# Linear attention's scores by 32-row products, state steps between projection products, and 32-column latent tiles in the first expert stage

## The reference, cut to what matters

```python
cum = jnp.cumsum(lc, axis=1)
inter = jnp.einsum('bchk,bhkv->bchv', qc * jnp.exp(cum), state)
scores = jnp.einsum('bihk,bjhk,bijhk->bhij', qc, kc, jnp.exp(diff))   # causal
intra = jnp.einsum('bhij,bjhv->bihv', scores, vc)
state = jnp.exp(last)[..., None] * state + jnp.einsum('bjhk,bjhv->bhkv', kc * jnp.exp(last[:, None] - cum), vc)
```

```python
hid = jax.nn.silu(jnp.einsum('becd,edf->becf', xs, w_gate)) * jnp.einsum('becd,edf->becf', xs, w_up)
y = jnp.einsum('becf,efd->becd', hid, w_down) * g[..., None].astype(h.dtype)
```

## Time and profile before

| | |
|---|---|
| median of 3 runs | 2052.12 us (2050.4 to 2054.34) |
| the profiled execution, its own time | 2049.58 us |
| its span | 2047.8 us |
| PE busy | 1906.9 us (93%) |
| DVE, ACT, POOL busy | 543.6, 461.7, 158.0 us |
| mean granted PE clock | 0.982 |
| first layer's experts (584 to 1130 us) | PE busy throughout |
| second layer's experts (1571 to 2030 us) | DMA at 426 to 427 GB/s |
| chain that ended last | PE 80%, DMA 11%, DVE 6% |

### The profile page before, as it was taken

The page is one execution under the profiler, slowest core; times in us unless marked ns, Lnnn a source line. Parts: engine busy times, 40 slices in busy tenths (PEclk is TensorE's granted clock), DMA queues, the critical chain, the costliest instruction groups (busy, mean ns, idle before and its releaser), DMA issues.

```text
span 2047.8 us, 24796 instructions
## 1 busy us (share of the span) xinstructions
PE 1906.9 (93%) x10438; PEld 880.8 (43%) x10438; DVE 543.6 (27%) x1212; ACT 461.7 (23%) x959; POOL 158.0 (8%) x225
## 2 busy tenths in 40 slices
PE   5999999999899999999999999989996998898886
PEld 3655545664333333333333555556642332332322
DVE  2021476662330000000001403466624010111113
ACT  4132213433311101110111404124432111110112
POOL 0000011110001010101111000011001000000000
PEclk9999999999899999999999999999997999999998
DMA  9312067002489999999999412130039999999996
GB/s 404 117 41 82 29 281 332 27 16 109 180 333 400 416 403 406 393 398 401 405 382 371 165 41 83 41 149 27 4 116 362 427 426 427 427 425 427 426 428 254
DMA packets 54279, 541.78 MB, mean 265 GB/s; under 512 B 6528, under 2 KB 8704, under 8 KB 23216
## 3 DMA queue, kind: packets, MB, share of 16 engines
q1 hardware_dynamic: 36704, 488.82, 57.8%
q0 software_dynamic: 17344, 51.72, 7.7%
q10 hardware_dynamic: 144, 0.01, 0.0%
HBM read 516.80 MB, written 23.72 MB: 264 GB/s over the span
## 4 chain that ended last, share of the span: by engine, by line
PE 80%; DMA 11%; DVE 6%; ACT 1%; issue 1%; SPq 0%; DVEq 0%; ACTq 0%
PE ps L2059 17%; PE ps L1670 10%; PE ps L2141 9%; PE ps L1895 7%; PE ps L2067 6%; PE ps L1646 5%; DMA ring<-in_wstream 5%; DMA work<-in_wstream 3%; DMA big<-in_wstream 3%; PE ps L1843 3%; PE ps L2148 3%; PE ps L2013 2%; PE ps L1593 2%; PE ps L1781 2%; PE ps L1638 1%; PE ps L1816 1%
## 5 line engine op out<-in xcount | busy, mean ns | idle before, releaser
L2059 PE MATMUL ps<-ring,work 128*64 128x512 f32 x1536 | 341.6, 596 | 14.3 <-DMA ring<-in_wstream 11.7
L1506 DVE TENSOR_TENSOR work<-glao,ps 128x512 f32<-128x512 f32 x31 | 21.3, 687 | 782.0 <-ACT glao L921 408.9
L1670 PE MATMUL ps<-hT,ring 128*128 128x512 f32 (+1 forms) x592 | 209.7, 513 | 4.9 <-issue 2.6
L2059 PEld LDWEIGHTS ps<-ring,work 128*64 128x64 f32 x1536 | 108.9, 137 | 241.5 <-issue 225.8
L2141 PE MATMUL ps<-big,work 128*64 128x512 f32 x704 | 164.7, 605 | 2.1 <-ACT work L881 2.1
L1670 PEld LDWEIGHTS ps<-hT,ring 128*128 128x128 f32 x592 | 113.2, 192 | 99.8 <-issue 89.9
L1895 PE MATMUL ps<-ring,hT 128*128 128x512 f32 x320 | 138.8, 592 | 0.0
L2067 PE MATMUL ps<-ring,work 128*32 128x512 f32 x1024 | 119.6, 597 | 0.0
L1646 PE MATMUL ps<-ring,hT 128*128 128x384 f32 (+3 forms) x384 | 110.9, 450 | 0.0
L736 ACT ACTIVATE work<-ps,work 128x512 f32<-128x512 f32 (+2 forms) x120 | 81.9, 684 | 83.7 <-DVE work L1202 48.5
L2059 PE MATMUL ps<-big,work 128*64 128x512 f32 x384 | 88.3, 605 | 13.3 <-DMA big<-in_wstream 13.3
(11 more groups left out here) (331 smaller groups left out, 2211.8 us busy)
## 6 DMA issues: line engine op xcount, KB each, us to landing
ring<-in_wstream SPq DMA_DIRECT2D x150, 2048.0 KB, 14.0
big<-in_wstream SPq DMA_DIRECT2D x68, 2048.0 KB, 18.7
hT<-in_wstream SPq DMA_DIRECT2D x12, 1024.0 KB, 31.5
work<-in_wstream SPq DMA_DIRECT2D x12, 1024.0 KB, 34.0
x_kept<-big POOLq DMA_DIRECT2D x14, 512.0 KB, 3.0
big<-x_kept POOLq DMA_DIRECT2D x12, 512.0 KB, 5.1
xn_lat<-big POOLq DMA_DIRECT2D x8, 512.0 KB, 3.8
big<-in_x_all SPq DMA_DIRECT2D x6, 512.0 KB, 6.6
```

Of the source, the lines that this page charges most:

```text
L1670: last = T.matmul(bank(n % 4, tn), uw[:, j * D + kc * P:j * D + kc * P + P], hTv[:, kc, t0:t0 + tn], start=kc == 0, stop=kc == KC - 1)
L2059: last = T.matmul(bank(m)[64 * h:64 * h + 64, :], XST[:, kc, e, 0:CAP_L], gate_up[j][kk][:, m * D + h * 512:m * D + (h + 1) * 512], start= ...
```

## The change

- **Scores.** The block-diagonal queries are gone. Per direction and head one product of 32 rows by 128 columns gives the head's scores; head h writes bank h, forward in its first 128 columns and backward in the next 128. `A_SB` has two copies, DVE signals `masked` after the two mask products, and PE starts the scores of the next tile at that signal. PE makes the state part ahead of the next tile's scores, and DVE copies the tile before out after the add. The modulation rows move to banks 4 and 5.
- **State steps.** PE makes state step i and the rotary product i behind item i of unit 4. On DVE a state step, the query arguments of one direction (after the first two steps) and one `rope` follow each other.
- **Ring.** `pe.drain()` and `ring_used` are gone. SP waits for the counters `proj`, `router_in` and `wo` that exist anyway.
- **32-column latent tiles.** In the first layer `up_lat` and `down_lat` make two products of 32 stationary columns in place of each one of 64.

```diff
+        A_SB = [w(GX, 512), w(GX + 1024, 512)]
-        QBLK = [w(q, 512) for q in (0, 512, 1024, GX + 1024)]
...
-                    sp.wait_ge(ring_used[lap(n)[0]], sum(lap(m)[0] == lap(n)[0] and m not in mod_units for m in ring_units if m <= n))
+                if n >= OUT_AT[l]:
+                    sp.wait_ge(sem("wo"), len(tiles(l)) + l * PER["wo"])
+                    return
+                unit = n - IN_AT[l]
+                sp.wait_ge(sem("proj"), n_items(l, unit + 1) + l * PER["proj"])
+                if unit == 2:
+                    sp.wait_ge(sem("router_in"), 1 + l * PER["router_in"])
...
+                for i in range(STEPS):
+                    step(i)
+                    if i < 2:
+                        query_args(l, i)
+                    rope(l, i)
...
-                queries(0)
+                by_head = v3(ps[:, 0:GLA_H * 512], GLA_H)
...
                     if i:
+                        dve.wait_ge(sem("A"), i + l * PER["A"])
+                    for d, (m, dst) in enumerate(((C_MF, A_SB[i % 2]), (C_MB, A_TMP))):
+                        last = V.tensor_tensor(v3(dst, GLA_H), by_head[:, :, d * P:(d + 1) * P],
+                                               cst[:, m:m + P].unsqueeze(1).broadcast_to([P, GLA_H, P]), ALU.mult)
+                    last.then_inc(sem("masked"), 1)
+                    dve.wait_ge(sem("masked"), i + 1 + l * PER["masked"])
+                    V.tensor_tensor(A_SB[i % 2], A_SB[i % 2], A_TMP, ALU.add).then_inc(sem("A"), 1)
...
-                        if unit == 4:
-                            rot(l, n - n_items(l, 4) - 1)
-                pe.drain().then_inc(ring_used[lap(g)[0]], 1)
+                        i = n - n_items(l, 4) - 1
+                        if unit == 4 and i < STEPS:
+                            state(l, i)
+                            rot(l, i)
...
+                    if i:
+                        pe.wait_ge(sem("masked"), i + l * PER["masked"])
                     for d in range(2):
-                        last = T.matmul(bank((4, 0)[i % 2] + d), E[3 * d + 1][:, ts[i] * P:(ts[i] + 1) * P], QBLK[2 * (i % 2) + d],
-                                        start=True, stop=True)
+                        for h in range(GLA_H):
+                            r = slice(DK * h, DK * h + DK)
+                            last = T.matmul(bank(h, P, d * P), E[3 * d + 1][r, c], E[3 * d][r, c], start=True, stop=True)
...
+                block = CAP_C if ctx_too else CAP_L
+                slot_blocks = [(h, b) for h in range(2) for b in range(0, CAP_L, block)]
...
-                                for h in range(2):
-                                    last = T.matmul(bank(m)[64 * h:64 * h + 64, :], XST[:, kc, e, 0:CAP_L],
+                                for h, b in slot_blocks:
+                                    r = CAP_L * h + b
+                                    last = T.matmul(bank(m)[r:r + block, :], XST[:, kc, e, b:b + block],
```

More of the change, by code:

```diff
@@ L1102, in gla_state, with step @@
                 hm = cst[:, C_HM:C_HM + GLA_H]
-                for i in range(NT - 1):
+                def step(i):
                     dve.wait_ge(sem("dS"), i + 1 + l * PER["dS"])
@@ L1114, in gla_state, with rope, query_args @@
                     dve.wait_ge(sem("state"), 2 * i + 2 + l * PER["state"])
[L1116 to L1125, removed]
+                for i in range(STEPS):
[3 more added lines that the diff above has]
+                    rope(l, i)
+            def rope(l, i):
+                b = [SK, SQ, SQ + 1, SQ + 2, SQ + 3][i]
+                dve.wait_ge(sem("rot"), i + 1 + l * PER["rot"])
+                V.tensor_tensor(ROT, bank(6 + i % 2), cst[:, C_SIN:C_SIN + LAT], ALU.mult)
+                link(V.tensor_tensor(FM[:, b, 0:LAT], FM[:, b, 0:LAT], cst[:, C_COS:C_COS + LAT], ALU.mult))
+                V.tensor_tensor(FM[:, b, 0:LAT], FM[:, b, 0:LAT], ROT, ALU.add).then_inc(sem("rope"), 1)
+                dve.wait_ge(sem("rope"), i + 1 + l * PER["rope"])
+            def query_args(l, d):
                 n = width(l)
@@ L1130, in gla_queries @@
                 dve.wait_ge(sem("keT"), 3 + l * PER["keT"])
[L1131 to L1139, removed]
+                c3 = v3(CUM[d], NT)[:, 0:nt, :]
+                mid = c3[:, :, P // 2:P // 2 + 1].broadcast_to([P, nt, P])
+                link(V.tensor_tensor(v3(E[3 * d + 2][:, 0:n], nt), c3, mid, ALU.subtract))
+                V.tensor_scalar(E[3 * d][:, 0:n], E[3 * d + 2][:, 0:n], 80.0, None, ALU.min).then_inc(sem("q_arg"), 1)
+                V.tensor_scalar(E[3 * d + 1][:, 0:n], E[3 * d + 2][:, 0:n], -80.0, -1.0, ALU.max, ALU.mult)\
+                    .then_inc(sem("q_arg"), 1)
+                dve.wait_ge(sem("q_arg"), 3 * d + 2 + l * PER["q_arg"])
+                V.tensor_copy(E[3 * d + 2][:, 0:n], CUM[d][:, 0:n]).then_inc(sem("q_arg"), 1)
+            def gla_queries(l):
+                n = width(l)
                 dve.wait_ge(sem("q_arg"), 6 + l * PER["q_arg"])
-                rope(l)
                 q = FM[:, GQ, 0:n]
@@ L1729, in gla_out @@
                 for i, t in enumerate(ts):
-                    if i + 1 < len(ts):
-                        scores(i + 1)
-                    if i == 0:
-                        mod_cols((1, 5)[l], GLA_ROW, bank(3))
                     c = slice(t * P, (t + 1) * P)
@@ L1926, in w_out @@
                                 last.then_inc(sem("xT"), 1)
-                for j in range(OUT_UNITS):
-                    pe.drain().then_inc(ring_used[lap(OUT_AT[l] + j)[0]], 1)
             def turn_lat(l):
@@ L2138, in down_lat @@
                         for kc in [4 * j + k for k in ks]:
-                            for g in range(2):
+                            for g, b in slot_blocks:
                                 h = g if ctx_too else g ^ e
-                                last = T.matmul(bank(6 if ctx_too else 3)[64 * g:64 * g + 64, :], HT[:, kc, 0:CAP_L],
+                                r = CAP_L * g + b
+                                last = T.matmul(bank(6 if ctx_too else 3)[r:r + block, :], HT[:, kc, b:b + block],
                                                 down[j][kc % 4 // 2][:, kc % 2, h * 512:(h + 1) * 512], start=kc == 0, stop=kc == KC - 1)
```

74 lines of the change are left out of this document (31 added, 43 removed).

## The result

| | before | after |
|---|---|---|
| median | 2051.26 us, 4 runs (2049.97 to 2054.34) | 2013.43 us, 4 runs (2007.03 to 2014.69) |
| profiled execution, its own time | 2049.58 us | 2012.75 us |
| its span | 2047.8 us | 2010.9 us |
| PE, DVE, ACT, POOL busy | 1906.9, 543.6, 461.7, 158.0 us | 1878.4, 531.4, 461.5, 158.0 us |

A forecast was written before the change was run, and what follows sets the result against it. PE was taken to set the pace, except in the second layer's experts (the stream) and where PE waits for DVE. Terms -14.5 - 9.6 - 11.5 - 1.4 = -37.0 us; 2052.1 - 37.0 = 2015, range about 2008 to 2031.

The forecast's parts named there:

- 32-column tiles: First layer's experts: fewer column-width changes between groups, -14.5 us (-15.2 at 0.1067 us per record, -12.8 at 0.1075).
- State steps: Unit 4, both layers: steps behind its items cost 4.3 us and no waiting, -4.8 us per layer, -9.6 in all.
- rival wait: Unit 4: PE waiting for state step i - 2; DVE at most 2 us behind in round 1, within what PE allows.
- Scores: Score tiles, both layers: PE-bound period of 2.8 to 2.9 us against 3.78, -6.8 and -4.9, taken as -11.5 us.
- I take 0.95: A tile's 16 score records: 0.95 us, between 0.73 if columns decide and 1.15 if the number of weight loads does.
- 0.73 us, period 2.6, -14: Better bound for the scores: 16 records in 0.73 us, DVE the limit at a 2.6 us period, -14 us.
- Drains: Unit ends: two standstills of 0.26 us and two of about 0.1 per layer go, -1.4 us, at least -0.5.
- The rival given 0.14: After the first layer's scores: denser tiles avoid the fall to 1.2 GHz, 3.1 us more gain, 2012; chance 0.14.
- Edges not being the cost: First layer's experts: every 32-column record costs 0.1116 us, +3.7 in place of -14.5, 2033 us; chance 0.10.
- the stream taking over: First expert stage: 404 GB/s is the limit, a pair of experts stays at 68.15 us, 2029.5 in all; chance 0.11.
- serial products: Scores: the 32-row products run one after the other without overlap of row groups, 2026 us; chance 0.10.
- The slower case: First layer's experts: loads of the doubled latent products are not hidden, up to +164 us, 2180; chance 0.04.

The follow-up runs named there:

- p1: The kernel before with only the 32-column latent tiles of the first layer's experts: 2037.26 us, ratio 0.9935.
- e5: The kernel before, with latent and context groups of units 0 and 1 taken in turns slice by slice, adding four width changes per expert: 2056.5 us, ratio 1.0032.
- e6: The changed kernel with latent and context groups of units 0 and 1 taken in turns slice by slice, both 32 wide: 2010.6 us, ratio 0.981.
- e10: The changed kernel with the next pair's gather transposes moved ahead of `up_ctx(3)` in odd experts, taking out two width changes: 2007.07 us, ratio 0.9795.
- p2: The kernel before with only the new order of state steps, query arguments and rotary products: 2041.29 us, ratio 0.996.
- p3: The kernel before with only the new scores by 32-row products: 2036.42 us, ratio 0.9932.
- e9: The changed kernel with all eight score products of a tile taken from the first head's 32 rows, one row group: 2049.83 us, ratio 0.9998.
- p4: The kernel before with only `pe.drain()` and `ring_used` removed and SP's new waits: 2048.17 us, ratio 0.9991.
- e7: The changed kernel with the score loops swapped, so both directions of a head follow each other in one row group: 2008.51 us, ratio 0.979.
- e8: The changed kernel with 32-column tiles in the second layer's experts too: 2011.81 us, ratio 0.9807.

## Why the prediction was right in the sum and off in its terms

- **32-column tiles** (predicted -14.5, p1 -12.9). The mechanism was right, the size was the lower of its two slopes: 32 records in 3.43 and 96 in 10.30 us are 0.1073 each, not 0.1067, and the pair's 66.54 lies at the slow end of 66.2 to 66.6. The four groups took 18.88, inside 18.8 to 18.9. e5, e6 and e10 settle that the edge is what was saved. In the profiled execution the stage gave only 11.3, since it began at 1.2 GHz (1.5 us).
- **State steps** (predicted -9.6, measured -4.8 and -4.8 in the two stretches, p2 -8.9 within 3 us). Right, and the rival wait (PE held by DVE in round 1) did not come: the pieces of the chain follow each other without a gap.
- **Scores** (predicted -11.5, measured -8.4 and -5.9, p3 -13.8). The mis-sized term. The step that failed is "I take 0.95" for the 16 records: it weighed columns against the number of weight loads and took a value between 0.73 and 1.15. Columns decide: at the same number of loads, 16 records took 1.15 us with 256 columns and 0.73 with 128, and the 0.42 between them is what 128 columns cost four groups at once (4 x 0.107). The 256 columns thus account for 0.85 of the 1.15; the rest, 0.30 by busy time, goes with the edge that e9 shows as a quarter of a microsecond by starts. (The prediction's 1.71 us for the earlier trace rows one after the other is the figure for 128 columns; for 256 it is 16 x 0.215 = 3.44. The reading that row groups overlap only gains by it.) So the bound "0.73 us, period 2.6, -14" was the case that came. The period was PE's to the end, DVE having 0.26 us per tile to spare, since its masks took 1.29, not 1.41.
- **Drains** (predicted -1.4, p4 -2.0, the traces -1.7 in each layer, so -3.4). The second mis-sized term. The prediction counted the time in which PE stands still at unit ends, 0.26 and about 0.1 us, and left out that the group behind each drain was some 0.24 us slower too (13.97 against 13.73).
- **The clock after the scores.** The rival given 0.14 came true in the first layer, p3 shows that the new scores are the cause, and it gave almost nothing. (In the second layer the clock fell behind the scores as before: 0.57 from 1357 to 1365 us before, and from 1320 to 1328 after.) In the earlier trace rows the clock was 0.61 in the mean; the same place of the changed kernel is at 1.00:

```profile
265.00:275.00 10.00, 8.15 (x67) 2.79 (x66) 9.29 (x10) 2.53 (x6) 7.00 (x6) 1.00 0.75 261
```

But DVE is busy for 9.29 of these 10 us: PE, now ahead, waits for ACT, and ACT for DVE, whose instructions of two columns (line 1212) take 2.29 us at 270.63 and 2.90 at 273.54 while POOL works on arrays of 1536 columns:

```profile
272.97 3.44 POOL L539 TENSOR_TENSOR glao<-glao,big 128x1536 f32<-128x1536 f32 x1
...
273.54 2.90 DVE L1212 TENSOR_SCALAR work<-work 128x2 f32<-128x2 f32 x1
...
274.02 0.66 PE L1820 MATMUL ps<-cst,work 128*128 128x128 f32 x4 [1.20 <-ACT work L742]
```

The median of this line's 20 instructions is 0.17 us. Of the rival's 3.1 us at most 0.9 came: attention and mixers took 166.94 us before and 166.08 after. Even these 0.9 need no full clock, since p1, with a shorter stretch at half clock in this place, takes 166.08 as well. The rival had counted what a slower PE loses, and not what stands beside PE at the full clock.

- **What the prediction left out.** The prediction took every stage between the changed ones as unchanged, and the profile has 2.1 us more in the router stage. 1.7 of them are one group (line 1965, before 1957), which takes 10.32 us at a clock of 0.57 (556 to 560 us) in place of 8.63. This is no effect of the change: profiles of other kernels with the same code there have 8.63 (e5, e7), 10.32 (p1 to p4) or 11.4 us (e8, e10). Where the clock falls in this stage differs between profiled runs, and the profile before was one of the good ones, as it was with the first group of the experts. The norms behind the first expert stage lost 1.65 us (26.53 to 24.88 between its end and the next projection), which was not followed up.
- **The other rivals.** Edges not being the cost is refuted by e5; the stream taking over, by PE at 100% and SP's waits; serial products, by e9 against the changed kernel. The slower case, loads that are not hidden, would have shown in p1, and in e8 as more PE time: neither does.

So that the sum fits to a microsecond is in part luck. Two terms were too small (scores by 2 to 3 us, drains by up to 2) and one too large (tiles, by 1.6), the norms gave 1.65 us that nobody had counted, and in the profiled execution some 3 us of stretches at 1.2 GHz and 2.0 us in the second layer stand against that.

## What to carry to other kernels

Before a product is changed in shape, look at its neighbours' shapes: equal tile widths in a row were worth 0.145 us per change of width saved, at twice the instructions and no more data. A full-height product over a block-diagonal array can be replaced by narrow ones if these are spread over different row groups; on one row group the same narrow products took the whole gain back, most of it by the clock (an estimated 28 us against 11). Look for the waits of PE and for what the clock does behind them: behind a wait of 3.34 us the router's 32 records took 4.90 us, and 2.79 when unused products had filled it, which with the same edit in the second layer was worth some 4 us. Before a difference of 2 us between two profiles is put down to a change, look whether it is one of these stretches.

## What the runs showed of the hardware that was not expected

- The granted clock fell to 0.50 for 41 us in e9 with PE busy throughout, by products of 32 rows in one row group. The changed kernel, with the same products spread over four groups, kept 1.00. Busy time in the profile is thus no sign that the clock will hold. Whether the rows in use or the weight loads decide was not tried.
- The order of products within a tile did not matter for the overlap of row groups (e7).
- The change of tile width costs 0.145 us in float32 at 2.4 GHz, in either direction (1.00 against 0.86 us, 1.87 against 1.72) and as much for a group of 32 records (3.57 against 3.43) as for one of 8, and the way into 32 rows and back 0.22 to 0.26 us for both (worked out by starts).
- A drain at a unit end costs its 0.26 us of standing still and about as much again in the group behind it (13.97 against 13.73 us, 1.7 us per layer in p4).
- DVE's instructions of two columns took 2.29 and 2.90 us beside POOL's elementwise work, against a median of 0.17 us. No run separates the two causes that this could have, a shared path or a wait that the profile does not show.
